# Neighbourhood attention: all turns of a step and the gated norm's factors behind the value products, and VectorE's copy a step later

## The reference, cut to what matters

```python
s_loc = jnp.einsum('bhcd,bhicjd->bhcij', qr, kw).astype(jnp.float32) * scale + bias
s_ctx = jnp.einsum('bhcd,bhnd->bhcn', qr, k_ctx).astype(jnp.float32) * scale
logits = jnp.concatenate([s_loc.reshape(B, H, GRID_W, n_loc), s_ctx], axis=-1)
p = jax.nn.softmax(logits, axis=-1).astype(v.dtype)
```

## Time and profile before

| what | value |
|---|---|
| device time, median of 3 runs | 3985.68 us (3982.15 to 3987.46) |
| the profiled execution, its own time | 3984.14 us |
| its span, first to last instruction | 3981.5 us |
| busy: TensorE | 3896.4 us (98%) |
| busy: VectorE | 1857.0 us (47%) |
| busy: ScalarE | 974.5 us (24%) |
| busy: GpSimd | 932.7 us (23%) |
| mean granted clock of TensorE | 0.991 |
| the stage of the change, 1722 to 1922 us: busy TensorE, VectorE, ScalarE | 188.5, 127.3, 110.0 us |

### The profile page before, as it was taken

The page is one execution under the profiler, slowest core; times in us unless marked ns, Lnnn a source line. Parts: engine busy times, 40 slices in busy tenths (PEclk is TensorE's granted clock), DMA queues, the critical chain, the costliest instruction groups (busy, mean ns, idle before and its releaser), DMA issues. The chain is left out here.

```text
span 3981.5 us, 48557 instructions
## 1 busy us (share of the span) xinstructions
PE 3896.4 (98%) x18394; PEld 2422.9 (61%) x18394; DVE 1857.0 (47%) x3907; ACT 974.5 (24%) x1837; POOL 932.7 (23%) x992
## 2 busy tenths in 40 slices
PE   8999999999999999989999999999999999999998
PEld 4788997786558568567544565656544444444447
DVE  3227884776252366646466322222566442223134
ACT  4224332333124311155224311111122010000000
POOL 0006773001111111133222112122132122222223
PEclk9999999999999999989999999999999999999999
DMA  5420003111220121132132112113243211111113
GB/s 195 156 85 11 8 9 73 37 47 53 85 77 27 53 64 57 51 113 91 48 99 64 43 38 80 42 57 103 98 147 122 80 32 42 48 48 43 42 46 102
DMA packets 113717, 270.25 MB, mean 68 GB/s; under 512 B 15623, under 2 KB 45177, under 8 KB 112398
## 3 DMA queue, kind: packets, MB, share of 16 engines
q1 hardware_dynamic: 106512, 251.81, 19.2%
q0 software_dynamic: 5920, 13.25, 1.3%
q10 hardware_dynamic: 1056, 2.10, 0.1%
HBM read 218.53 MB, written 50.87 MB: 68 GB/s over the span
## 5 line engine op out<-in xcount | busy, mean ns | idle before, releaser
L452 PE MATMUL upper_banks<-sbuf 128*128 128x512 f32 (+1 forms) x2016 | 771.3, 545 | 1.5 <-issue 1.1
L3360 PE MATMUL upper_banks<-sbuf 128*128 128x512 f32 x1400 | 616.6, 596 | 5.5 <-ACT sbuf L3637 4.5
L452 PEld LDWEIGHTS upper_banks<-sbuf 128*128 128x128 f32 x2016 | 382.4, 190 | 388.7 <-issue 373.8
L3360 PEld LDWEIGHTS upper_banks<-sbuf 128*128 128x128 f32 x1400 | 263.0, 191 | 317.9 <-issue 308.3
L2502 PE MATMUL gla_prod<-sbuf 128*128 128x512 f32 x560 | 247.6, 593 | 0.3 <-DVE sbuf L2534 0.3
L608 DVE TENSOR_TENSOR sbuf<-upper_banks,sbuf 128x512 f32<-128x512 f32 (+1 forms) x140 | 81.9, 585 | 283.2 <-PE upper_banks L452 282.6
L404 POOL TENSOR_TENSOR sbuf<-sbuf 128x512 f32<-128x512 f32 x36 | 46.7, 1298 | 655.6 <-DMA sbuf<-in_w_mlp_out 307.4
L1039 PE MATMUL mla_banks<-sbuf 128*128 128x128 f32 x1344 | 176.0, 278 | 5.5 <-POOL sbuf L878 4.3
L2502 PEld LDWEIGHTS gla_prod<-sbuf 128*128 128x128 f32 x560 | 104.5, 192 | 119.9 <-issue 117.4
L1662 PE MATMUL mls_banks<-sbuf 128*128 128x512 f32 x392 | 175.1, 593 | 0.3 <-DVE sbuf L2079 0.3
L1039 PEld LDWEIGHTS mla_banks<-sbuf 128*128 128x128 f32 x1344 | 162.9, 192 | 10.5 <-POOL sbuf L878 7.2
(11 more groups left out here) (565 smaller groups left out, 6657.0 us busy)
## 6 DMA issues: line engine op xcount, KB each, us to landing
sbuf<-in_l_w_in SPq DMA_DIRECT2D x59, 512.0 KB, 4.0
sbuf<-in_w_in SPq DMA_DIRECT2D x52, 512.0 KB, 4.5
sbuf<-in_w_mlp_out SPq DMA_DIRECT2D x40, 512.0 KB, 3.6
sbuf<-in_w_mlp_in SPq DMA_DIRECT2D x32, 512.0 KB, 3.6
sbuf<-in_l_w_mod SPq DMA_DIRECT2D x24, 512.0 KB, 6.4
scratch_gates<-sbuf SPq DMA_DIRECT2D x48, 256.0 KB, 2.0
sbuf<-in_l_w_mod SPq DMA_DIRECT2D x8, 1024.0 KB, 16.4
sbuf<-in_l_w_out SPq DMA_DIRECT2D x16, 512.0 KB, 4.0
```

The lines of the kernel that those rows point to most:

```text
L452: last = nc.tensor.matmul(bank_of(n, c)[:, 0:wd], lw[:, k * P:(k + 1) * P], right_operand(c, base, tw, k, o, wd, to), start=k == 0 and c i ...
L3360: last = nc.tensor.matmul(pb, lw[:, k * P:(k + 1) * P], rhs, start=k == 0 and c in ("P1", "P2", "P5"), stop=k == 3, skip_group_check=True)
```

## The change

On TensorE the last turns of step i move from behind the scores to behind `weigh(i - 1)`, so that all turns of an iteration stand together. The two factor products leave `weigh` and become a function of their own, `gates(i)`, that runs between the last turns of i and the first turns of i + 1, one iteration earlier than before; it waits for the outputs of step i - 2, which read the same bank. On VectorE the copy and the inverse of a step move one iteration later: iteration i now ends with copy and inverse of i in place of i + 1.

```diff
+            def gates(i):
+                if 0 <= i - GATE0 < 16:
+                    pe.wait_ge(ginv, 1)
+                    pe.wait_ge(oev, i - 1)
+                    for t in range(2):
+                        c = 2 * (i - GATE0) + t
+                        nc.tensor.matmul(banks[:, 6 + i % 2, (2 + t) * P:(3 + t) * P], gcol[:, c:c + 1].broadcast_to([P, P]), ident[:],
+                                         start=True, stop=True)
+
             def weigh(i):
...
                 pe.wait_ge(inverted, i + 1)
-                if 0 <= i - GATE0 < 16:
-                    pe.wait_ge(ginv, 1)
-                    for t in range(2):
-                        c = 2 * (i - GATE0) + t
-                        nc.tensor.matmul(B[:, (2 + t) * P:(3 + t) * P], gcol[:, c:c + 1].broadcast_to([P, P]), ident[:],
-                                         start=True, stop=True)
                 for h in range(2):
...
             for i in range(-2, NS + 1):
                 if i + 2 < NS:
                     scores(i + 2)
-                if 0 <= i < NS:
-                    turn(i, range(2, nb[i]))
                 if i == -2:
                     gla_sums(2)
                     gla_sums(3)
                 if i >= 1:
                     weigh(i - 1)
+                if 0 <= i < NS:
+                    turn(i, range(2, nb[i]))
+                    gates(i)
                 if 0 <= i + 1 < NS:
                     turn(i + 1, range(2))
...
                     nc.vector.reciprocal(gcol[:], gcol[:]).then_inc(ginv, 1)
-                if 0 <= i + 1 < NS:
-                    copy(i + 1)
-                    inverse(i + 1)
+                if 0 <= i < NS:
+                    copy(i)
+                    inverse(i)
```

## The result

The change makes the kernel slower: 4141.51 us median of 4 runs (4138.76 to 4148.39) against 3985.77 us of before; ratio 1.0393, interval 1.0379 to 1.0407. The profiled execution took 4140.75 us, 156.6 more than the one of before. 4156 was forecast, in a range of 4094 to 4195.

What follows compares the result with a forecast made beforehand. TensorE, busy for 98% of the span, was taken to bound the kernel. 3984.1 us plus 110 for serialized steps and ends plus 61 for the lowered clock gave 4155, 4156 on the median's scale; range 4094 to 4195.

Steps and rivals of the forecast that it cites:

- The chain: Attention stage: scores, products, spreads, turns, row maximum, outputs, copy, first turns run serially; 9.70 us even, 8.71 odd steps; +107.0.
- from outputs to copy: VectorE's outputs up to the start of its copy, in each step of the stage; taken as 0.79 us.
- +1.5 at the start: First iteration: row maximum and copy change places, so the next scores start 1.5 us after their present time.
- +1.4: Last two steps, without scores: outputs and copy come onto the path twice, less turns and waits that go; estimated +1.4 us.
- (a): VectorE's wait at L4721: the row maximum writes the probabilities' buffer of step i, so waits for all its turns.
- (b): TensorE's wait at L4500: a turn waits for its bank, that is for the copy two batches earlier.
- rival 3: The row maximum's wait for the turns is over in time; only outputs and copy join the path: +32, 4017 us; chance 0.04.
- The clock: Pauses of 3.3 to 4.3 us in each step lower TensorE's granted clock; 2.1 us a step, 29 times: +61.
- mean of five: Mean low-clock busy time after five single pauses in the earlier trace, 4.2 us, half of it counted as lost per step.
- the row without a fall: The one of five earlier pauses, 2.4 us long, after which TensorE's clock stayed at 1.00, counted as 0.
- Rival 1: TensorE's clock stays at 2.4 GHz, so only the +110 us of serial steps and ends counts: 4095 us; chance 0.12.
- rival 2: TensorE's clock stays at 1.2 GHz through the stage, doubling its part of each step: 4239 us; chance 0.06.

Runs made afterwards that it cites:

- second filled run: The change with 17 (even step) or 14 (odd step) unneeded extra products behind each step's last turns; 4090.87 us, ratio 1.0270 to the kernel before.
- copy late: The kernel before with only VectorE's copy and inverse moved one iteration later, TensorE's order as before; 4058.63 us, ratio 1.0182.
- third buffer: The change with a third buffer for the probabilities, so the row maximum no longer waits for the last turns; 4012.68 us, ratio 1.0066 to the kernel before.
- turns late: The change with VectorE's copy and inverse put back one iteration earlier, TensorE's order as in the change; 4039.69 us, ratio 1.0131 to the kernel before.

## Why the prediction was right

- **The chain.** For the 29 steps +107.0 was worked out, and +102.8 measured with the clock held up. Steps of 9.70 and 8.71 came out at 9.51 and 8.60. The term that was mis-sized most is the one from outputs to copy: 0.79 was taken from one of the last steps, and it is 0.57 in the steps here (1778.09 to 1778.66). The eight turns were put in with their whole row of 1.09, while the next scores start 0.99 after them, and factors add 0.38 to 0.39 to a step (9.89 and 8.99) in place of 0.47. At the end +1.4 was an estimate, and +2.4 came; the +1.5 at the start lies ahead of the stage as it is measured here, and no row tells it apart.
- **Waits (a) and (b).** Each was opened by itself: 4013 us without (a) (rival 3 priced that case at 4017), 4011 without (b). Both are needed, as the chain says.
- **The clock.** +61 was taken, 58 measured, or 2.0 us a step in place of 2.1. That the size came so near is in part luck: the mean of five holds the zero of the row without a fall, but the fall came in every one of the 29 steps, and its 2.0 on the mean is less than that of the four rows that had one (2.6). A granted clock of 0.80 in the stage lay within the 0.6 to 0.85 named as the sign. Rival 1 (clock stays up, 4095) is the second filled run at 4091; rival 2 (clock down throughout) fell with the rows at full clock in each step. The Trainium skill's loop rule ("TensorE: Matmul & The Clock Gate", section "HAM oscillation — how this bites in real kernels") has a loop in which a wait in each turn throttles each turn. The trace agrees: 29 pauses of 3.48 to 4.64 us, slow scores behind each of them, a mean clock of 0.80. The 76 us that the prediction put beside it, from the four rows, are further off than the mean of five.
- **The rest.** Of the 14 us between forecast and median some 4 are the chain's, 3 the clock's, and 6 lie outside of the stage, which no step of the forecast touched.
- **The factors.** They were taken as free under cover and 0.64 without it. Left in place they cost 12.8 us. Not foreseen: moved alone, they make the stage 2.9 us shorter.

## What to carry to other kernels

Before moving an instruction in an order written by hand, follow each wait that stays in place to what it now stands behind: here a buffer with two halves and two banks closed a ring round the engines, and its length (sum of durations from rows) gave the step to within 3%. A loop that leaves TensorE a pause in each turn, of 3.5 to 4.6 us here, pays for the pause and again for the work after it; price both. A pair of moves can be harmful in each half and worse together, so time the halves.

## What the runs showed of the hardware that was not expected

- A single pause of 2.4 us left the clock at 1.00 in the earlier trace rows, but recurring ones of 1.25 to 2.2 us lowered it: with the copy late the clock was 0.90 in the part with factors (1803.57 to 1940.98), while recurring pauses of 0.9 to 1.7 us (third buffer) left it at 0.99 over the stage.
- The length of the pause alone does not decide it. In the same run, copy late, the steps without factors have longer pauses, 1.50 and 2.57 us, and from 1781.22 to 1803.57 they ran at 1.00. With the turns late, pauses of 1.5 to 1.7 us stand in nearly every step, and only five steps are slow. Why was not tried.
- The two factor products of a step (four instructions) take 0.54 us right behind turns and 0.64 behind value products, and each of the three groups round them starts 0.05 to 0.1 us earlier in the new place. Why was not tried.
